# Rewriting the work order of a latent-attention and retention stage, and moving its rotations from VectorE to GpSimd

## The chip, the cores and the metric

The kernel runs on one core of a Trainium2 chip. The metric is the time of one execution in microseconds (us); the median of three executions of the kernel before is 1068.57 us (1067.65 to 1068.61). In the rows PE is TensorE, PEld its weight loads, DVE VectorE, ACT ScalarE, POOL GpSimd and SP the engine that issues most DMAs.

## The reference

The reference runs one sequence of 256 rows by 1024 features through seven pieces: a convolution mixer, a feed-forward, a sliding-window attention, two feed-forwards, a mixed stage, and a last feed-forward with a final norm. The change lies in the mixed stage:

```python
n = rms_norm(h, mix_norm[l])
proj = n @ w_in[l]
c_q, c_kv, k_pe, r_q, r_k, r_v, r_g = jnp.split(proj, SPLIT_POINTS, axis=-1)
a = mla_group(c_q, c_kv, k_pe, ...)     # 8 heads, softmax over 256 keys
r = retention_group(r_q, r_k, r_v, r_g, ...)  # 8 heads, decay in place of softmax
h = h + jnp.concatenate([a, r], axis=-1) @ w_o[l]
```

`mla_group` projects a latent of 256 + 128 features to queries, keys and values, rotates a part of them, and does softmax attention. `retention_group` rotates its queries and keys (the first half of every head times cosine and sine, minus and plus the second), multiplies scores by a decay, normalises each head over its features and gates the result.

## The kernel before

**Products.** The 256 rows are two tiles t = 0, 1 of 128. All weights come as one stream of chunks of 128 x 1024 floats (512 KB). Every product is exact to f32 by three passes: a chunk is split into a high part (ACT, `split_high`, L1044) and a low part (DVE, `split_low`, L1326), and so is the activation. Tile 0 multiplies a chunk first and waits for its split; tile 1 multiplies it last and frees its slot.

**Ring and raw buffers.** Split chunks live in a ring of 12 slots (`RING`), unsplit ones in 4 raw buffers (`RAW`). Once the chunk of a slot is freed, a step `R` splits the chunk that comes 12 later into it. SP loads a raw buffer again as soon as DVE has split what was in it, so at most four chunks are loaded ahead of the splits.

**Order.** Nothing is scheduled at run time. `walk` names the steps in one order, each engine walks through it and takes the steps that it has a part in, and works them off strictly in that order; semaphores join the engines. Where a step stands in `walk_latent` so decides what it stands behind on each of its engines. `freed` is the list of freed chunks, `refill(step, freed, n)` puts n steps `R` there.

**The head loop** (before: 797.5 to 831.3 us of the span). The MLA heads go in 8 pairs v:

- MS(v): PE multiplies the scores into bank pG[v % 2] (L1914); DVE takes the row maximum `mx` from there (L1576) and scales it to `negm` (L1579).
- ME(v): ACT takes the exponent into `mp` (L1249), two instructions with a sum each.
- MN(v): DVE takes the reciprocal of the sums (L1584) and multiplies `mp` by it (L1586).
- MPT(v): PE turns `mp` into bank pT (L1661), ACT copies it to `mpT` (L1256).
- MPV(v): PE multiplies it with the values (L1933).

Beside them run projections X(i, t, c), six matmuls of 128x512 each (L1656 to L1658): i = 3 are the retention's values, i = 4 its gate. VC takes the mean of the values (reduction on DVE, subtraction on POOL, L1000), `decay` makes the decay tables (ACT, POOL L1005), MAT splits the attention's output, RT turns the rotated queries and keys.

**The rest of the stage.** RS, RM and RPV are the retention's scores, their product with the decay (DVE, L1612) and the product with the values; SQ, VAR, GNvar, GNout the norm; GT turns the gate; RY multiplies it in (DVE `yo`, L1632; ACT splits off the high part), RL gives the low part (DVE, L1642). O(t, kt) are the output products, eight for each tile; O(t, 4..7) need RL(t). RROPE(t, part) is one rotation of 128 x 512 (part 0 queries, 1 keys): on DVE four multiplications into `ttmp` and two additions back into `rqk` (L1544 to L1550).

**The last feed-forward** takes blocks b: G(t, b) is the gate and up product over four chunks, T(t, b) turns the activated tile, D(t, b) is the down product over two. After T(0, 0) stands a refill of everything still in `freed`.

Of the kernel before, what the change touches and what calls it, by code (L numbers as in the profile page):

```python
# [31 lines left out]
ALU = mybir.AluOpType  # L32
# [3 lines left out]
P = 128  # L36
# [113 lines left out]
def refill(step, freed, n=None):  # L150

    for _ in range(len(freed) if n is None else min(n, len(freed))):
        step("R", freed.pop(0), 1, 0)
# [255 lines left out]
def walk_latent(step, freed, open_end):  # L409


    def project(i, t, c):
        step("X", i, t, c)
        if t == 1:
            freed.append(C_X[i] + c)

    def projects(i, t, cs=range(4)):
        for c in cs:
            project(i, t, c)
            if t == 1 and len(freed) > 1:  # L420
                refill(step, freed, 1)
# [30 lines left out]
    projects(3, 0)  # L452
    step("MT", 1)
    step("VC", 0)
# [3 lines left out]
    beside = [(3, 1, c) for c in range(1, 4)] + [(4, 0, c) for c in range(4)] + [(4, 1, 0)]  # L458
    project(*beside.pop(0))
    step("ME", 0)  # L460
    for v in range(1, 9):
        step("MN", v - 1)
        if v < 8:
            step("MS", v)
        refill(step, freed, v % 2)
        if v < 8:
            step("MPT", v - 1)
            project(*beside.pop(0))
            step("ME", v)
        else:  # L470
            step("RT", 0)
            step("MPT", v - 1)
            project(4, 1, 1)
        if v == 4:
            step("VC", 1)
        if v % 2 == 0:
            step("decay", v // 2 - 1)
        step("MPV", v - 1)
        if v == 7:
            step("MAT", 0)  # L480
    step("gate", 0)
    step("RT", 1)
    step("decay", 4)
    project(4, 1, 2)
    refill(step, freed, 1)
# [3 lines left out]
    project(4, 1, 3)  # L489
    refill(step, freed, 1)  # L490
# [5 lines left out]
    output(0, 0)  # L496
    refill(step, freed, 1)
# [5 lines left out]
    output(0, 1)  # L503
    step("MAT", 1)
    refill(step, freed, 1)
# [4 lines left out]
    output(0, 2)  # L510
    refill(step, freed, 1)
# [3 lines left out]
    step("SQ", 1)  # L515
    refill(step, freed, 1)
    output(0, 3)
    step("VAR", 1)
    step("GNvar", 1)
    step("GNout", 0)  # L520
    output(1, 0)
    refill(step, freed, 1)
    step("GNout", 1)
    output(1, 1)
    step("GT", 0)
    step("RY", 0)
    output(1, 2)
    step("RL", 0)
    step("GT", 1)
    step("RY", 1)  # L530
    output(1, 3)
    step("RL", 1)
    refill(step, freed, 4)
# [60 lines left out]
def build(nc, x_in, stream, consts_in, table_in, pos_in, posts_in, out):  # L594
    with ExitStack() as ctx:
# [172 lines left out]
        dm_exp, dm_ready = sem("dm_exp"), sem("dm_ready")  # L768
# [105 lines left out]
        def _(pool):  # L874
# [126 lines left out]

            def decay(hd, ph):

                pool.wait_ge(dm_exp, 3 * (hd + 1))
                pool.tensor_tensor(dm[hd][:, P:2 * P], dm[hd][:, P:2 * P], dtmp[hd % 2][:], ALU.mult).then_inc(dm_ready, 1)  # L1005
# [15 lines left out]
            steps = {f.__name__: f for f in (start, parts, finish, tail, rope, S, LAT, VC, decay, GNvar)}  # L1021
# [289 lines left out]
        def _(ve):  # L1311
# [218 lines left out]
            def RROPE(t, part, ph):  # L1530

                if t == 0 and part == 0:
                    ve.wait_ge(sincos_ready, 2)
                ve.wait_ge(x_out[t], 2 + part)
                z = rqk[t][:, 512 * part:512 * part + 512].rearrange("p (a f) -> p a f", f=HD)
                co, si = (x[:, t, :].unsqueeze(1).broadcast_to([P, 8, RHALF]) for x in (cos2, sin2))
                x1, x2 = z[:, :, 0:RHALF], z[:, :, RHALF:HD]
                if t or part:
                    ve.wait_ge(rrope_done[t if part else 0], 1 if part else 2)
                rotate(x1, x2, co, si, [x[:] for x in ttmp]).then_inc(rrope_done[t], 1)  # L1540

# [98 lines left out]
            def RL(t, ph):  # L1640
# [5 lines left out]
                         rope=rope, QKT=QKT, S=S, N=N, AT=AT, LAT=LAT, U=U, RROPE=RROPE, MT=MT, MS=MS, MN=MN, VC=VC, RT=RT, RM=RM, GNvar=GNvar, GNout=GNout,  # L1646
# [483 lines left out]
```

## Time and profile before

| what | value |
|---|---|
| median of three executions | 1068.57 us |
| the profiled execution's own time | 1068.61 us |
| its span, first to last instruction | 1066.8 us |
| PE busy / PE weight loads busy | 99% / 81% of the span |
| DVE / ACT / POOL busy | 62% / 53% / 8% |
| mean granted TensorE clock | 0.997 of full speed |
| HBM read | 186 MB, 175 GB/s over the span |

A busy share of PE is the time in which any matmul is in flight; matmuls overlap, so a wait shows only where PE has run dry. In a timeline a group xN is N instructions of one form, its duration from the first start to the last end. A bracket such as [1.39 <-DVE mp L1586] says that the engine sat idle 1.39 us and that this instruction released it.

### The profile page before, as it was taken

Reading aid. Unit: us, or ns where it says so; the run is one execution under the profiler, and the core shown is the slowest. Engines: PE = TensorE matmul, PEld = TensorE weight load, DVE = VectorE, ACT = ScalarE, POOL = GpSimd, SP = SyncE. Lnnn points to the kernel's source line nnn. Section 1 sums busy time; section 2 is a strip of 40 time slices with the busy share of each in tenths; the row PEclk is TensorE's granted clock in tenths of the full one; section 3 lists DMA queues with packets and bytes.
Section 4 is the critical chain, followed back from the end, with each engine's and each line's share of the span. In section 5 each row is a group of like instructions: output and inputs, shape, how many; then the busy total and the mean of one; then the engine's idle time right before and its main releaser. Section 6 shows DMA issues by size and latency. Waiting matters only on the chain.

```text
span 1066.8 us, 14789 instructions
## 1 busy us (share of the span) xinstructions
PE 1050.9 (99%) x5023; PEld 862.2 (81%) x5023; DVE 658.3 (62%) x956; ACT 566.7 (53%) x917; POOL 83.4 (8%) x170
## 2 busy tenths in 40 slices
PE   9999999999999999999999999999999999999997
PEld 6998888888877788888888888888886688888886
DVE  5867754645787765454576545466696664655544
ACT  5755644544677754454465445445567744444542
POOL 0034000000022040000000000000011110000001
PEclk9999999999999999999999999999999999999999
DMA  8573655546562364654656455565542353646541
GB/s 339 190 240 120 222 172 198 191 163 218 176 212 85 119 203 165 204 186 168 215 180 202 160 210 180 174 211 183 178 158 80 119 168 109 209 164 217 169 147 40
DMA packets 51883, 187.80 MB, mean 176 GB/s; under 512 B 5808, under 2 KB 5952, under 8 KB 51840
## 3 DMA queue, kind: packets, MB, share of 16 engines
q1 hardware_dynamic: 50688, 183.79, 51.0%
q0 software_dynamic: 864, 3.07, 1.0%
q8 instruction: 27, 0.44, 0.2%
q10 hardware_dynamic: 288, 0.37, 0.1%
q14 instruction: 16, 0.13, 0.0%
HBM read 186.15 MB, written 1.05 MB: 175 GB/s over the span
## 4 chain that ended last, share of the span: by engine, by line
PE 90%; DVE 6%; ACT 2%; issue 1%; POOL 0%; POOLq 0%; DVEq 0%; ACTq 0%
PE pG L1656 17%; PE pG L1658 17%; PE pG L1657 17%; PE pD L1656 11%; PE pD L1658 11%; PE pD L1657 11%; PE pT L1661 3%; DVE w_low L1326 2%; PE pG L1678 1%; PE pG L1661 1%; PE pT L1799 1%; PE pG L1914 0%; PE pD L1661 0%; ACT w_high L1044 0%; PE pD L1667 0%
## 5 line engine op out<-in xcount | busy, mean ns | idle before, releaser
L1326 DVE TENSOR_TENSOR w_low<-raw,w_high 128x1024 fp32r<-128x1024 f32 x340 | 410.8, 1225 | 121.6 <-ACT w_high L1044 108.1
L1044 ACT ACTIVATE w_high<-raw 128x1024 fp32r<-128x1024 f32 x340 | 352.8, 1055 | 76.7 <-PE pG L1658 66.2
L1656 PE MATMUL pG<-w_high,xTh 128*128 128x512 f32 (+1 forms) x816 | 319.9, 392 | 0.1
L1658 PE MATMUL pG<-w_high,xTl 128*128 128x512 f32 (+1 forms) x816 | 312.5, 383 | 0.0
L1657 PE MATMUL pG<-w_low,xTh 128*128 128x512 f32 (+1 forms) x816 | 312.1, 382 | 0.0
L1658 PEld LDWEIGHTS pG<-w_high,xTl 128*128 128x128 f32 x816 | 153.1, 188 | 28.0
L1657 PEld LDWEIGHTS pG<-w_low,xTh 128*128 128x128 f32 x816 | 153.6, 188 | 25.6
L1656 PEld LDWEIGHTS pG<-w_high,xTh 128*128 128x128 f32 x816 | 153.2, 188 | 25.6 <-DVE xTl L1359 0.3
L1656 PE MATMUL pD<-w_high,aTh 128*128 128x512 f32 x384 | 150.8, 393 | 0.0
L1658 PE MATMUL pD<-w_high,aTl 128*128 128x512 f32 x384 | 149.9, 390 | 0.0
L1657 PE MATMUL pD<-w_low,aTh 128*128 128x512 f32 x384 | 149.4, 389 | 0.0
L1129 ACT ACTIVATE gate<-pG,stat 128x256 f32<-128x256 f32 x104 | 49.3, 475 | 166.1 <-PE pG L1658 165.4
L1149 ACT ACTIVATE aTh<-pT 128x256 fp32r<-128x256 f32 x88 | 33.7, 383 | 150.7 <-PE pT L1661 150.7
L1465 DVE TENSOR_TENSOR aTl<-pT,aTh 128x256 fp32r<-128x256 f32 x88 | 37.4, 425 | 119.0 <-ACT aTh L1149 119.0
L1446 DVE SCALAR_TENSOR_TENSOR act<-pG,stat,gate 128x256 f32<-128x256 f32 x88 | 42.4, 481 | 94.8 <-ACT gate L1129 94.6
L1658 PEld LDWEIGHTS pD<-w_high,aTl 128*128 128x128 f32 x384 | 72.1, 188 | 15.1
L1657 PEld LDWEIGHTS pD<-w_low,aTh 128*128 128x128 f32 x384 | 72.2, 188 | 14.1
L1656 PEld LDWEIGHTS pD<-w_high,aTh 128*128 128x128 f32 x384 | 72.1, 188 | 14.1
L1656 PE MATMUL pD<-w_high,xTh 128*128 128x512 f32 (+1 forms) x160 | 65.5, 409 | 1.1 <-issue 1.1
L1658 PE MATMUL pD<-w_high,xTl 128*128 128x512 f32 (+1 forms) x160 | 62.6, 391 | 0.0
L1657 PE MATMUL pD<-w_low,xTh 128*128 128x512 f32 (+1 forms) x160 | 62.3, 390 | 0.0
L1656 PEld LDWEIGHTS pD<-w_high,xTh 128*128 128x128 f32 x160 | 30.2, 189 | 10.0 <-issue 4.9
(266 smaller groups left out, 811.5 us busy)
## 6 DMA issues: line engine op xcount, KB each, us to landing
raw<-in_stream SPq DMA_DIRECT2D x340, 512.0 KB, 4.4
post<-in_posts POOLq DMA_DIRECT2D x5, 512.0 KB, 4.8
early<-in_stream SPq DMA_DIRECT2D x4, 512.0 KB, 12.4
first_w<-in_stream SPq DMA_DIRECT2D x3, 512.0 KB, 5.9
h<-in_x SPq DMA_DIRECT2D x2, 512.0 KB, 5.5
out<-hg SPq DMA_DIRECT2D x3, 256.0 KB, 2.3
consts<-in_consts POOLq DMA_DIRECT2D x1, 417.0 KB, 4.5
out<-hg ACTq DMA_DIRECT2D x1, 256.0 KB, 2.7
```

What stands on the lines that cost most here:

```text
L1044: sc.activation(w_high[:, slot(static):slot(static) + CHUNK], raw_of(static), ACT.Copy).then_inc(w_high_done, 1)
L1129: sc.activation(gate[t][:], pG[t][:, 0:256], ACT.Copy if ph.mixer else ACT.Silu, scale=rr[t]).then_inc(gate_ready[t], 1)
L1149: sc.activation(aTh[t][:].rearrange("p k r -> p (k r)"), pT[t][:, 0:256], ACT.Copy).then_inc(ah_ready[t], 1)
L1326: ve.tensor_tensor(w_low[:, slot(static):slot(static) + CHUNK], raw_of(static), w_high[:, slot(static):slot(static) + CHUNK].bitcast(F32), ...
L1446: ve.scalar_tensor_tensor(act[t][:], pG[t][:, 256:512], rr[t], gate[t][:], ALU.mult, ALU.mult).then_inc(act_ready[t], 1)
L1465: ve.tensor_tensor(aTl[t][:].rearrange("p k r -> p (k r)"), pT[t][:, 0:256], aTh[t][:].rearrange("p k r -> p (k r)").bitcast(F32), ALU.sub ...
L1656: pe.matmul(dst, ah, hi, start=start, stop=False)
L1657: pe.matmul(dst, ah, lo, start=False, stop=False)
L1658: return pe.matmul(dst, al, hi, start=False, stop=stop)
L1661: return pe.transpose(dst, src, ident)
L1678: mm = pe.matmul(pG[t][:, 0:MIX.cols], hg[t][:, kt * P:(kt + 1) * P], first_w[:, kt * MIX.cols:(kt + 1) * MIX.cols], start=kt == 0, stop=k ...
L1799: mm = pe.matmul(pT[p][:, P * keys * x:P * keys * (x + 1)], qT[t][part, 4 * a + first + x, :], kT[part, a, 0:P * keys], start=True, stop=True)
```

## The change

The change has five parts.

1. RROPE moves from DVE to POOL, 24 instructions with the same operands. The wait for the sine and cosine tables on DVE goes with it.
2. In the head loop MS runs two pairs ahead of MN and MPT, where it ran one ahead. PE's round was MS(v), MPT(v-1), X, MPV(v-1); it is MPT(v), X, MS(v+2), MPV(v-1). A second refill stands ahead of the loop, before MN(0), and the first VC before the second MT. X(4, 1, 0) and X(4, 1, 1) leave the loop.
3. The retention part is ordered anew: three projections beside RT, RS and RPV, RL(0) after both RY, VAR(1) followed by O(0, 3).
4. There the refills are fewer: two single ones and one of two, where there were seven single ones and one of four (three were left to do). What is left over moves behind T(0, 0) of the last feed-forward.
5. A semaphore `rot_part` counts POOL's four multiplications.

```diff
--- before.py
+++ after.py
@@ -450,87 +450,85 @@
     step("exp_table",)
     freed += [C_U, C_U + 1, C_U + 2]
     projects(3, 0)
+    step("VC", 0)
     step("MT", 1)
-    step("VC", 0)
     project(3, 1, 0)
     refill(step, freed, 1)
     step("MS", 0)
-    beside = [(3, 1, c) for c in range(1, 4)] + [(4, 0, c) for c in range(4)] + [(4, 1, 0)]
+    step("ME", 0)
+    step("MS", 1)
+    beside = [(3, 1, c) for c in range(1, 4)] + [(4, 0, c) for c in range(4)]
     project(*beside.pop(0))
-    step("ME", 0)
-    for v in range(1, 9):
-        step("MN", v - 1)
-        if v < 8:
-            step("MS", v)
+    refill(step, freed, 1)
+    for v in range(8):
+        if v < 7:
+            step("ME", v + 1)
+        step("MN", v)
+        step("MPT", v)
+        for _ in range(min(1, len(beside))):
+            project(*beside.pop(0))
+        if v < 6:
+            step("MS", v + 2)
+        if v >= 1:
+            step("MPV", v - 1)
+        if v == 3:
+            step("VC", 1)
+        if 2 <= v < 6:
+            step("decay", v - 2)
+        if v == 6:
+            step("MAT", 0)
         refill(step, freed, v % 2)
-        if v < 8:
-            step("MPT", v - 1)
-            project(*beside.pop(0))
-            step("ME", v)
-        else:
-            step("RT", 0)
-            step("MPT", v - 1)
-            project(4, 1, 1)
-        if v == 4:
-            step("VC", 1)
-        if v % 2 == 0:
-            step("decay", v // 2 - 1)
-        step("MPV", v - 1)
-        if v == 7:
-            step("MAT", 0)
+    step("RT", 0)
     step("gate", 0)
+    step("MPV", 7)
+    project(4, 1, 0)
     step("RT", 1)
+    project(4, 1, 1)
     step("decay", 4)
-    project(4, 1, 2)
-    refill(step, freed, 1)
     step("decay", 5)
     step("RS", 0)
     step("RM", 0)
-    project(4, 1, 3)
-    refill(step, freed, 1)
+    project(4, 1, 2)
     step("decay", 6)
     step("RPV", 0)
     step("RS", 1)
     step("RM", 1)
     step("decay", 7)
-    output(0, 0)
-    refill(step, freed, 1)
+    project(4, 1, 3)
     step("RPV", 1)
     step("RS", 2)
     step("gate", 1)
     step("SQ", 0)
     step("RM", 2)
-    output(0, 1)
     step("MAT", 1)
-    refill(step, freed, 1)
+    output(0, 0)
     step("RPV", 2)
     step("RS", 3)
     step("RM", 3)
     step("silu",)
-    output(0, 2)
-    refill(step, freed, 1)
+    output(0, 1)
     step("VAR", 0)
     step("GNvar", 0)
     step("RPV", 3)
     step("SQ", 1)
+    step("GNout", 0)
     refill(step, freed, 1)
-    output(0, 3)
+    output(0, 2)
     step("VAR", 1)
     step("GNvar", 1)
-    step("GNout", 0)
-    output(1, 0)
+    output(0, 3)
+    step("GNout", 1)
     refill(step, freed, 1)
-    step("GNout", 1)
-    output(1, 1)
+    for kt in range(3):
+        output(1, kt)
     step("GT", 0)
     step("RY", 0)
-    output(1, 2)
-    step("RL", 0)
+    output(1, 3)
     step("GT", 1)
     step("RY", 1)
-    output(1, 3)
+    step("RL", 0)
     step("RL", 1)
-    refill(step, freed, 4)
+    refill(step, freed, 2)
     for kt in range(4, 8):
         output(0, kt)
     step("tail", 0, C_INDEX)
@@ -765,7 +763,7 @@
...
@@ -999,6 +997,22 @@
                 z = rv[t][:].rearrange("p (a f) -> p a f", f=HD)
                 pool.tensor_tensor(z, z, gn[t][:, 0, :].unsqueeze(2).broadcast_to([P, RET_HEADS, HD]), ALU.subtract).then_inc(vc_ready, 1)
 
+            def RROPE(t, part, ph):
+
+                pool.wait_ge(x_out[t], 2 + part)
+                z = rqk[t][:, 512 * part:512 * part + 512].rearrange("p (a f) -> p a f", f=HD)
+                co, si = (x[:, t, :].unsqueeze(1).broadcast_to([P, 8, RHALF]) for x in (cos2, sin2))
+                x1, x2 = z[:, :, 0:RHALF], z[:, :, RHALF:HD]
+                if t or part:
+                    pool.wait_ge(rrope_done[t if part else 0], 1 if part else 2)
+                pool.tensor_tensor(ttmp[0][:], x1, co, ALU.mult).then_inc(rot_part, 1)
+                pool.tensor_tensor(ttmp[1][:], x2, si, ALU.mult).then_inc(rot_part, 1)
+                pool.tensor_tensor(ttmp[2][:], x1, si, ALU.mult).then_inc(rot_part, 1)
+                pool.tensor_tensor(ttmp[3][:], x2, co, ALU.mult).then_inc(rot_part, 1)
+                pool.wait_ge(rot_part, 4 * (2 * t + part + 1))
+                pool.tensor_tensor(x1, ttmp[0][:], ttmp[1][:], ALU.subtract)
+                pool.tensor_tensor(x2, ttmp[2][:], ttmp[3][:], ALU.add).then_inc(rrope_done[t], 1)
+
             def decay(hd, ph):
 
                 pool.wait_ge(dm_exp, 3 * (hd + 1))
@@ -1018,7 +1032,7 @@
                 pool.wait_ge(end_m, 2)
                 pool.tensor_tensor(rr[1], ms[1], half_neg[:, 0:1], ALU.pow).then_inc(end_r, 1)
 
...
 
             def step(name, *args, ph=None):
@@ -1527,18 +1541,6 @@
                 ve.wait_ge(lath_ready, t + 1)
                 ve.tensor_tensor(latTl[:], latf[:], latTh[:].bitcast(F32), ALU.subtract).then_inc(latT_ready, 1)
 
-            def RROPE(t, part, ph):
-
-                if t == 0 and part == 0:
-                    ve.wait_ge(sincos_ready, 2)
-                ve.wait_ge(x_out[t], 2 + part)
-                z = rqk[t][:, 512 * part:512 * part + 512].rearrange("p (a f) -> p a f", f=HD)
-                co, si = (x[:, t, :].unsqueeze(1).broadcast_to([P, 8, RHALF]) for x in (cos2, sin2))
-                x1, x2 = z[:, :, 0:RHALF], z[:, :, RHALF:HD]
-                if t or part:
-                    ve.wait_ge(rrope_done[t if part else 0], 1 if part else 2)
-                rotate(x1, x2, co, si, [x[:] for x in ttmp]).then_inc(rrope_done[t], 1)
-
             def rotate(x1, x2, co, si, tmp):
 
                 chain(ve.tensor_tensor(tmp[0], x1, co, ALU.mult))
@@ -1643,7 +1645,7 @@
                                  xTh[t][:, 4:8, :].rearrange("p k r -> p (k r)").bitcast(F32), ALU.subtract).then_inc(catT_ready[t], 1)
 
...
 
```

What this does to the instructions is shown at three places. Names carry the buffer's digit (pG0, mp1) and a running number.

DVE at the start of the head loop, before: the maximum of pair 0 (from pG0), MN(0), the maximum of pair 1, and the chunk split after it.

```order
L1576 TENSOR_REDUCE mx0_67<-pG0 128x2 [waits ms_psum]
L1579 TENSOR_SCALAR negm0_69<-mx0_67 128x2 [waits ve_chain]
L1584 RECIPROCAL lrec0_73<-lsum0_71 128x2 [waits mp_ready]
L1586 TENSOR_TENSOR mp0_133<-mp0_133,lrec0_73 128x512 [waits ve_chain]
L1576 TENSOR_REDUCE mx0_67<-pG1 128x2 [waits ms_psum]
L1579 TENSOR_SCALAR negm0_69<-mx0_67 128x2 [waits ve_chain]
L1326 TENSOR_TENSOR w_low_51<-raw_49,w_high_50 128x1024 [waits w_high_done]
L1584 RECIPROCAL lrec0_73<-lsum0_71 128x2 [waits mp_ready]
```

DVE at the same place, now:

```order
L1578 TENSOR_REDUCE mx0_67<-pG0 128x2 [waits ms_psum]
L1581 TENSOR_SCALAR negm0_69<-mx0_67 128x2 [waits ve_chain]
L1578 TENSOR_REDUCE mx0_67<-pG1 128x2 [waits ms_psum]
L1581 TENSOR_SCALAR negm0_69<-mx0_67 128x2 [waits ve_chain]
L1340 TENSOR_TENSOR w_low_51<-raw_49,w_high_50 128x1024 [waits w_high_done]
L1586 RECIPROCAL lrec0_73<-lsum0_71 128x2 [waits mp_ready]
L1588 TENSOR_TENSOR mp0_133<-mp0_133,lrec0_73 128x512 [waits ve_chain]
L1578 TENSOR_REDUCE mx0_67<-pG0 128x2 [waits ms_psum]
L1581 TENSOR_SCALAR negm0_69<-mx0_67 128x2 [waits ve_chain]
```

MN(0), which is RECIPROCAL and mp0, stood behind one maximum; now it stands behind two and behind a chunk split, and MN(1) will stand behind the maximum of pair 2.

PE around MPT(2) (pT0 from mp0), before: MPV(1), MS(3), MPT(2).

```order
L1933 MATMUL pD0<-mpT1_137,mv0_125 64x128 [waits mpT_ready]
L1933 MATMUL pD0<-mpT1_137,mv0_125 64x128
L1933 MATMUL pD0<-mpT1_137,mv1_126 64x128 x2
L1914 MATMUL pG1<-mkT_120,mqT_117 128x256 [waits mp_ready]
L1914 MATMUL pG1<-mkT_120,mqT_117 128x256
L1661 MATMUL pT0<-consts_61,mp0_133 128x128 [waits mpT_ready,mn_ready]
L1661 MATMUL pT0<-consts_61,mp0_133 128x128 x3
```

PE at the same place, now: MS(3), MPV(0), MPT(2).

```order
L1916 MATMUL pG1<-mkT_120,mqT_117 128x256 [waits mp_ready]
L1916 MATMUL pG1<-mkT_120,mqT_117 128x256
L1935 MATMUL pD0<-mpT0_136,mv0_125 64x128 [waits mpT_ready]
L1935 MATMUL pD0<-mpT0_136,mv0_125 64x128
L1935 MATMUL pD0<-mpT0_136,mv1_126 64x128 x2
L1663 MATMUL pT0<-consts_61,mp0_133 128x128 [waits mpT_ready,mn_ready]
L1663 MATMUL pT0<-consts_61,mp0_133 128x128 x3
```

MS(3) and MPT(2) are as close as before. What the rows alone don't say is that on DVE MN(2) stood before the maximum of pair 3 and now stands behind it.

DVE at the start of the last feed-forward, before: the preparation of tile 1, T(0, 0), one chunk split, and the activation of G(0, 1).

```order
L1359 TENSOR_TENSOR xTl1_55<-hg1_85,xTh1_53 128x512 [waits xh_ready1] x2
L1465 TENSOR_TENSOR aTl0_80<-pT0,aTh0_78 128x256 [waits ah_ready0]
L1326 TENSOR_TENSOR w_low_51<-raw_49,w_high_50 128x1024 [waits w_high_done]
L1446 SCALAR_TENSOR_TENSOR act0_88<-pG0,stat_63,gate0_86 128x256 [waits gate_ready0]
L1465 TENSOR_TENSOR aTl0_80<-pT0,aTh0_78 128x256 [waits ah_ready0]
```

DVE at the same place, now:

```order
L1373 TENSOR_TENSOR xTl1_55<-hg1_85,xTh1_53 128x512 [waits xh_ready1] x2
L1479 TENSOR_TENSOR aTl0_80<-pT0,aTh0_78 128x256 [waits ah_ready0]
L1340 TENSOR_TENSOR w_low_51<-raw_49,w_high_50 128x1024 [waits w_high_done] x7
L1460 SCALAR_TENSOR_TENSOR act0_88<-pG0,stat_63,gate0_86 128x256 [waits gate_ready0]
L1479 TENSOR_TENSOR aTl0_80<-pT0,aTh0_78 128x256 [waits ah_ready0]
```

Seven chunk splits stand between T(0, 0) and the activation of G(0, 1), where one stood.

## Rows read from the trace of the kernel before

**Rows 1.** The page, part 1: busy us, share of the span and instructions of each engine.

```profile
PE 1050.9 (99%) x5023; PEld 862.2 (81%) x5023; DVE 658.3 (62%) x956; ACT 566.7 (53%) x917; POOL 83.4 (8%) x170
```

**Rows 2.** The waits of PE, 740 to 900 us: us in total, times, longest.

```profile
PE pT L1661 <- DVE mp L1586: 3.0, 3, 1.4
PE pD L1656 <- issue: 1.1, 1, 1.1
PE pT L1973 <- DVE sd L1612: 0.7, 1, 0.7
PE pG L1656 <- DVE mkT L1570: 0.6, 1, 0.6
```

**Rows 3.** Stretches: length; busy us by engine; granted clock, DMA share, GB/s.

```profile
797.50:831.30 33.80, 30.84 (x190) 22.63 (x190) 22.39 (x43) 21.84 (x60) 4.79 (x6) 1.00 0.24 79
```

**Rows 4.** Timeline of PE, head loop: start, us, work, idle before.

```profile
802.24 0.66 PE L1661 MATMUL pT<-consts,mp 128*128 128x128 f32 x4 [1.39 <-DVE mp L1586]
...
804.21 0.66 PE L1933 MATMUL pD<-mpT,mv 128*64 128x128 f32 x8
804.80 1.13 PE L1914 MATMUL pG<-mkT,mqT 96*128 96x256 f32 x4
...
807.70 0.66 PE L1933 MATMUL pD<-mpT,mv 128*64 128x128 f32 x8
```

**Rows 5.** Timeline of DVE over the same rounds.

```profile
801.29 0.17 DVE L1584 RECIPROCAL lrec<-lsum 128x2 f32<-128x2 f32 x1 [1.09 <-ACT mp L1249]
801.49 0.69 DVE L1586 TENSOR_TENSOR mp<-mp,lrec 128x512 f32<-128x512 f32 x1
802.10 0.68 DVE L1576 TENSOR_REDUCE mx<-pG 128x2 f32<-128x512 f32 x1
802.82 0.17 DVE L1579 TENSOR_SCALAR negm<-mx 128x2 f32<-128x2 f32 x1
802.90 1.22 DVE L1326 TENSOR_TENSOR w_low<-raw,w_high 128x1024 fp32r<-128x1024 f32 x1
...
805.97 0.69 DVE L1576 TENSOR_REDUCE mx<-pG 128x2 f32<-128x512 f32 x1 [0.60 <-PE pG L1914]
```

**Rows 6.** Timeline of ACT over the same rounds.

```profile
800.24 0.47 ACT L1249 ACTIVATE mp<-pG,negm 128x256 f32<-128x256 f32 x1 [3.02 <-DVE negm L1579]
...
801.15 1.05 ACT L1044 ACTIVATE w_high<-raw 128x1024 fp32r<-128x1024 f32 x1
802.93 0.60 ACT L1256 ACTIVATE mpT<-pT 128x512 f32<-128x512 f32 x1 [0.73 <-PE pT L1661]
```

**Rows 7.** Timeline of POOL, 797 to 818 us.

```profile
798.23 1.95 POOL L1000 TENSOR_TENSOR rv<-rv,gn 128x512 f32<-128x512 f32 x1 [15.54 <-DVE gn L1594]
...
815.88 1.04 POOL L1000 TENSOR_TENSOR rv<-rv,gn 128x512 f32<-128x512 f32 x1 [4.96 <-DVE gn L1594]
```

**Rows 8.** Timeline of DVE beside the second of these.

```profile
816.29 1.17 DVE L1586 TENSOR_TENSOR mp<-mp,lrec 128x512 f32<-128x512 f32 x1
```

**Rows 9.** Tile ttmp, one of six lines of a rotation: ns min/median/max.

```profile
L1544 DVE TENSOR_TENSOR ttmp<-rqk,trig x4: 413/418/419, 760.0 to 793.8; 128x256 f32<-128x256 f32 x4
```

**Rows 10.** Timeline of DVE before the last product of the stage.

```profile
860.00 0.69 DVE L1642 TENSOR_TENSOR xTl<-yo,xTh 128x512 fp32r<-128x512 f32 x1 [0.70 <-ACT xTh L1303]
860.61 0.68 DVE L1632 TENSOR_TENSOR yo<-roS,pG 128x512 f32<-128x512 f32 x1
```

**Rows 11.** Timeline of PE, 856 to 858 us.

```profile
856.77 0.63 PE L1657 MATMUL pD<-w_low,xTh 128*128 128x512 f32 x1
857.20 0.63 PE L1658 MATMUL pD<-w_high,xTl 128*128 128x512 f32 x1
```

**Rows 12.** Timeline of PE at the start of the last feed-forward.

```profile
880.15 0.44 PE L1661 MATMUL pT<-consts,act 128*128 128x128 f32 x2 [0.21 <-DVE act L1446]
```

**Rows 13.** Timeline of DVE at the same place.

```profile
883.82 1.23 DVE L1326 TENSOR_TENSOR w_low<-raw,w_high 128x1024 fp32r<-128x1024 f32 x1 [0.52 <-ACT w_high L1044]
```

**Rows 14.** Tile raw, 775 to 790 us: from a load's issue to its landing.

```profile
DMA to landing us min/median/max: 3.3/4.4/5.2
```

More of the change, by code:

```diff
@@ L767, in build @@
         rT_psum, rqT_ready, rkT_ready = sem("rT_psum"), sem("rqT_ready"), sem("rkT_ready")
-        dm_exp, dm_ready = sem("dm_exp"), sem("dm_ready")
+        dm_exp, dm_ready, rot_part = sem("dm_exp"), sem("dm_ready"), sem("rot_part")
         rs_psum, sd_ready, rpv_done = sem("rs_psum"), sem("sd_ready"), sem("rpv_done")
@@ L1019, in finish @@
                 pool.tensor_tensor(rr[1], ms[1], half_neg[:, 0:1], ALU.pow).then_inc(end_r, 1)
-            steps = {f.__name__: f for f in (start, parts, finish, tail, rope, S, LAT, VC, decay, GNvar)}
+            steps = {f.__name__: f for f in (start, parts, finish, tail, rope, S, LAT, VC, RROPE, decay, GNvar)}
             in_loop = ("G", "D", "T", "Y", "R")
@@ L1645, in _ @@
             steps = dict(start=start, fill=fill, R=refill, turn=turn, parts=parts, second=second, finish=finish, tail=tail, join=join, G=G, T=T, Y=Y,
-                         rope=rope, QKT=QKT, S=S, N=N, AT=AT, LAT=LAT, U=U, RROPE=RROPE, MT=MT, MS=MS, MN=MN, VC=VC, RT=RT, RM=RM, GNvar=GNvar, GNout=GNout,
+                         rope=rope, QKT=QKT, S=S, N=N, AT=AT, LAT=LAT, U=U, MT=MT, MS=MS, MN=MN, VC=VC, RT=RT, RM=RM, GNvar=GNvar, GNout=GNout,
                          MAT=MAT, RY=RY, RL=RL)
```

## The prediction

> **What bounds the kernel now.** I read the page's busy shares first: PE is in flight for 99% of the span, everything else for at most 81% [rows 1]. A change that leaves PE's matmuls as they are, as this one does, can only take away or add waits of PE, so I read next who PE waited for around the stage. From 740 to 900 us that is 5.4 us in all: 3.0 for the normalised probabilities of MN in the head loop, 1.1 put down to issue (the wait of O(1, 0) for the first value of the norm, a DVE result that VAR(1) had just asked for), 0.7 for RM, 0.6 for `mkT` [rows 2]. That is all that the new order can win. Then I read the timelines of PE, DVE and ACT over two rounds of the head loop, to see how much room stands between a result and its use.
>
> The round takes 3.49 us (804.21 to 807.70) [rows 4]. After MS(v) the chain is: maximum, exponent, MN, MPT. The maximum starts 1.17 us after MS does (804.80, 805.97) [rows 4, 5]; DVE's next instruction starts 0.80 us after it (802.10 to 802.90) [rows 5]; the exponents start at 800.24 and leave ACT free 0.91 us later; MN's reciprocal starts at 801.29, 1.05 us after the exponents, and MPT 0.95 us after it [rows 4 to 6]. The old order hides this chain nearly whole because DVE does MN(v-1) before it must wait for MS(v).
>
> **The head loop.** The new PE round is MPT(v), X, MS(v+2), MPV(v-1), MPT(v+1). On ACT the distance of two pairs does what it seems to do, the exponents are early. But DVE works in program order, and there MN(v+1) stands behind the maximum of pair v+2, which waits for MS(v+2) of the same PE round. So a round is:
>
> - MPT and X, 1.97 us (802.24 to 804.21) [rows 4]
> - MS(v+2) to its maximum, 1.1 us (an estimate: the 1.17 of above, less what PE loses in changing over from an MPV, which MS no longer follows)
> - the maximum to the next DVE instruction, 0.80; reciprocal to MPT(v+1), 0.95 [rows 4, 5]
>
> That is 4.83 us, with 0.6 of it covered by MPV(v-1) on PE. When a refill stands between the two (v = 1, 3, 5), add the step of a chunk split, 1.22 less the 0.08 by which DVE's instructions overlap: 5.97 us. The high part on ACT is ready for it, but for v = 1, where ACT copies the values first (0.15). For v = 3 VC adds 0.79, and its subtraction on POOL another 0.6 (below).
>
> Ahead of the loop: MS(0) at 0, maximum at 1.1 to 1.17, exponents from 2.1, ACT free at 3.0, the high part of the extra refill until 4.1, its low part on DVE until 5.25, MPT(0) at 6.2. Rounds v = 0, 2, 4: 3 x 4.83 = 14.5. Rounds 1, 3, 5: 3 x 5.97 + 0.15 + 0.79 + 0.6 = 19.45. From MPT(6) to MPT(7) nothing is left to multiply, and MAT stands before MN(7) on DVE: copy visible after 0.69 (802.24, 802.93) [rows 4, 6], two ACT copies 1.1, DVE 0.61, MN 0.95, together 3.35. MPT(7) is so at 43.5. MPT, MPV(6), RT and MPV(7) add 2.5, and two X that the old loop held, 3.1: 49.1 against 33.8 of the old stretch with the same work [rows 3]. **Term A: +15.3 us.** It hangs on no duration that the trace lacks, only on the order. Its ends: without the lock and with chunk splits that DVE finds time for, 11; with splits that come late from ACT, 18.
>
> **The retention part.** Gone are the issue wait (VAR(1) is followed by O(0, 3), 1.5 us of work), RM's wait (no split stands before RM(0)), and the low-clock stretch that followed VAR: there matmuls start every 0.43 us (856.77, 857.20) [rows 11] where 0.23 is usual, so that X takes 2.6 and not 1.4 to 1.6; eight matmuls and the turn beside them cost 1.4. New is a wait before O(0, 4): its low part RL(0) now stands behind RY(1), which waits for GT(1). From GT(1): 0.69 to `yo`, 0.61 to the next instruction, 0.69 for RL [rows 10], 2.0 in all, with 0.4 of GT on PE: 1.6. **Term B:** -1.1 - 0.7 - 1.4 + 1.6 = **-1.6 us** (-3.2 if the low part is early, 0 if the clock falls here again).
>
> **The rotations.** DVE is rid of 24 instructions of 0.42 us [rows 9], 10 us. That frees the one place where they bind: U(1) waits 0.6 for `mkT`, whose copies stood behind a rotation and four splits. POOL's cost for 128x256 isn't in the trace. The nearest row is 1.04 us for 128x512 with two inputs [rows 7]; half of that, 0.52, and the whole are the ends, and I take 0.7. A rotation is then 4.2 us (3.1 to 6.2). The last starts when `rqk` of tile 1 is out, near 787, and is over by 795; its first readers are ME(1), after 800, and RT. So it is covered. The cost is elsewhere. POOL's subtraction took 1.95 us beside DVE and 1.04 alone, and the DVE product beside the second took 1.17 where 0.69 is usual [rows 5, 7, 8]: the two wait for each other. The last rotation so meets DVE's U(1), on which MT(1) waits; at most two of its six instructions should fall on it. **Term C:** -0.6 (-1 to +3.6).
>
> The Trainium skill has a rule that speaks against this part: in SBUF — State Buffer, "SBUF: two separate sides", the port pair of VectorE and GpSimd is an exclusive lock, held for a whole instruction, that a VectorE instruction with two SBUF inputs needs. The trace agrees (1.17 against 0.69). By it alone, what moved to POOL gives DVE nothing back wherever DVE is busy.
>
> **The last feed-forward.** G(0, 1) starts after the turn at 880.15, at about 880.35 [rows 12]. It needs chunks 4 to 7 of the phase, a chunk each 1.4 us (six matmuls). Now only chunk 4 is split by then; 5 to 11 come behind T(0, 0). The first split there starts at 883.82 [rows 13] and is done at 885.05, where PE wants it at 881.75: 3.3 us. The next come each 1.14 and keep up. But only four loads run ahead: the load of chunk 9 waits for the split of 5, lands 3.3 to 4.4 later [rows 14], and with two split steps of 1.05 and 1.22 is ready at 891 to 892, wanted at 890.6. And the activation of G(0, 1) stands behind all seven on both engines: the last is split near 893.5, T(0, 1) could start at 892.3 to 893. That gives 0.4 to 1.4 and 1.4 more. **Term D: +5.5 us** (5 to 6.2; 2 if loads land sooner). Behind it the ring is as full as it was.
>
> **The clock.** The granted clock fell once in this stage, to 1.2 of 2.4 GHz, after VAR's small matmuls and the wait of 1.1 us, and an X in it cost 1.2 more [rows 2, 11]. The waits of 1.4 in the loop did not make it fall. The new waits are longer and closer: 2.9, 2.1, 2.8, 1.5, 4.0, 1.5, 2.7 and 2.4 in the loop, 3.3 at the end. I take it that the longest four or five each cost such a stretch, and that in each about 0.9 falls on the path. **Term E: +4 us** (0 to +10).
>
> **Sum.** 15.3 - 1.6 - 0.6 + 5.5 + 4 = 22.6 on the profiled execution's 1068.6 (span 1066.8 and 1.8 around it, the median of the runs is the same to 0.1): 1091.2, said as 1091.
>
> **The rivals.**
>
> - *Scores two ahead hide the softmax after all.* For it speaks that MS and its MPT lie two rounds apart. The 3.0 go, with B and C that is -5.2, and D gives 5.5 back: 1068.9; with D at nothing, 1063. It needs that MN(v+1) doesn't wait for MS(v+2), so it decides at one point: whether DVE starts a reciprocal before the maximum that stands ahead of it. In the trace no DVE instruction does so. The Trainium skill says the same of VectorE (TensorE: Matmul & The Clock Gate, "Architectural detail: the array is 16× 32×32, not 1× 128×128": its queue is strictly first in, first out). Chance 0.05.
> - *The rotations on POOL bind.* If each of the six instructions of the last rotation holds DVE's U(1) up, MT(1) is 4.2 late and C is +3.6, and those beside the splits delay a chunk: 1096 to 1097. Chance 0.12.
> - *The clock stays low.* If every wait brings a low stretch, nine of them at 1.2, E is 10 to 11: 1098. Chance 0.12.
> - *The splits find room.* If ACT's high parts come while DVE waits for MS, the odd rounds cost 4.83: A falls by 3.4, and with E near 1 it is 1085. But a split behind the maximum can't start before it. Chance 0.04.
>
> **How the numbers follow.** The forecast's own case has 0.67, around 1091. With A at 11 and E at 0 it is 1083, and a little less with D at 5: 1082 is the low end. 1099 takes in the second and third rival. What a measurement here can tell from no change is about 0.2%, 2 us. Faster needs the first rival without D: 0.03; within 0.2%, the same with D: 0.02; slower 0.95.
>
> **What would show it.** MPT of the head loop should wait for DVE `mp` eight times, 18 to 20 us in total, rounds alternating near 4.8 and 6.0; the loop up to RT(0) should take about 44.5 us at full clock. A wait of 1.6 before O(0, 4) for `xTl` L1644. At the last feed-forward, PE waits for `w_low` about 3.3 us, then for `act` 1.4. The granted clock below 0.95 in the loop. POOL's rotation instructions 0.5 to 1.9 us, no wait of PE for `rqk`. I am wrong if the loop's waits are near 3 us in all, or if PE waits for `w_low` nowhere.

## The result and the profile after

The changed kernel takes 1096.84 us (median of four runs, 1096.28 to 1097.33) against 1068.59 (1067.65 to 1069.51): a ratio of 1.0264, 95% interval 1.0247 to 1.0282, so 28 us slower. The forecast was 1091 with a range of 1082 to 1099. The direction and the mechanism of the head loop held, and the sum was 5.6 us short. The experiments below are mostly about these 5.6.

First the page of the changed kernel: its span, part 1, and the granted clock in 40 slices.

```profile
span 1095.3 us, 14788 instructions
PE 1059.1 (97%) x5023; PEld 867.6 (79%) x5023; DVE 658.3 (60%) x932; ACT 567.8 (52%) x917; POOL 105.1 (10%) x194
PEclk9999999999999999999999999999988999999999
```

The work is that of before [rows 1], but for 24 instructions that went from DVE to POOL. DVE's busy time didn't fall with them. The waits of PE from 740 to 930 us, which answer to [rows 2]:

```profile
PE pT L1663 <- DVE mp L1588: 17.5, 8, 3.8
PE pG L1658 <- DVE w_low L1340: 3.1, 1, 3.1
PE pT L1663 <- DVE act L1460: 2.3, 2, 2.1
PE pG L1663 <- DVE mq L1552: 1.7, 1, 1.7
PE pD L1658 <- DVE xTl L1644: 1.4, 1, 1.4
```

These are 26.0 us where before there were 5.6 (the 5.4 of [rows 2] and 0.2 ahead of T(0, 0)). From kernel to kernel MT(0) starts up to 1.5 us earlier or later, behind work that the edits don't touch, so I compare distances between landmarks and not positions. In the timeline of PE, these rows are the landmarks:

```profile
777.90 0.60 PE L1663 MATMUL pG<-consts,mq 128*96 128x128 f32 x4
...
799.36 1.96 PE L1916 MATMUL pG<-mkT,mqT 96*128 96x256 f32 x8
...
851.67 0.60 PE L1658 MATMUL pD<-w_high,xTh 128*128 128x512 f32 x1
...
882.81 0.50 PE L1658 MATMUL pD<-w_high,xTh 128*128 128x512 f32 x1 [1.38 <-DVE xTl L1644]
...
901.41 0.44 PE L1663 MATMUL pT<-consts,act 128*128 128x128 f32 x2 [0.21 <-DVE act L1460]
...
906.35 0.67 PE L1658 MATMUL pG<-w_high,xTh 128*128 128x512 f32 x1 [3.11 <-DVE w_low L1340]
...
917.13 0.44 PE L1663 MATMUL pT<-consts,act 128*128 128x128 f32 x2 [2.08 <-DVE act L1460]
```

They are MT(0), MS(0), the first X after MPV(7), O(0, 4), T(0, 0), G(0, 1) and T(0, 1). The same landmarks in the other kernels:

| stretch, us | before | after | clock kept up and late splits gone (`e8`) | new order (`e7`) |
|---|---|---|---|---|
| MT(0) to MS(0) | 20.4 | 21.5 | 21.4 | 20.4 |
| MS(0) to the end of the head loop, equal work | 33.8 | 55.4 | 48.6 | 31.3 |
| from there to T(0, 0) | 48.8 | 46.6 | 47.5 | 45.2 |
| T(0, 0) to T(0, 1) | 8.5 | 15.7 | 8.5 | 8.5 |

(To make the work of the loop equal, 1.55 us are added to it and taken from the next stretch for each X that a kernel does behind it: two after and in `e8`, one in `e7`. Where RT(1) or an X follows MPV(7), its start and the end of MPV(7) differ by up to 0.1 us.) The column after, less the column before, is 1.1 + 21.6 - 2.2 + 7.2 = 27.7; the other 0.8 of the difference of the spans lies ahead of MT(0). Behind T(0, 1) both take 178.2.

The lock that was forecast can be read off DVE's timeline, here where the clock is full:

```profile
808.45 0.69 DVE L1578 TENSOR_REDUCE mx<-pG 128x2 f32<-128x512 f32 x1 [3.00 <-PE pG L1916]
809.17 0.17 DVE L1581 TENSOR_SCALAR negm<-mx 128x2 f32<-128x2 f32 x1
809.25 0.16 DVE L1586 RECIPROCAL lrec<-lsum 128x2 f32<-128x2 f32 x1
809.44 0.69 DVE L1588 TENSOR_TENSOR mp<-mp,lrec 128x512 f32<-128x512 f32 x1
```

The exponents for this reciprocal were done at 804.3, but DVE stood idle for 3.00 us in front of the maximum of pair 2, behind which the reciprocal of pair 1 stands. And at half clock, on PE:

```profile
818.86 0.63 PE L1659 MATMUL pD<-w_low,xTh 128*128 128x512 f32 x1
819.28 0.63 PE L1660 MATMUL pD<-w_high,xTl 128*128 128x512 f32 x1
```

A matmul starts every 0.43 us, as in [rows 11]. The stretch from MS(0) to the end of MPV(7), in a view of stretches (length; busy us by engine; granted clock, DMA share, GB/s):

```profile
799.36:851.67 52.31, 34.81 (x179) 25.95 (x179) 22.55 (x42) 23.92 (x61) 4.18 (x5) 0.84 0.15 51
```

The mean of 0.84 says that the clock was at its half level for about a third of the loop; finer stretches show four pieces.

### The profile page after: what moved, and what is told of

Same layout as the page of the kernel before. It is cut to its first block, busy times and chain, and to the rows that moved or that the text cites. A ratio compares the mean times of both kernels' runs of the same rounds, so it can differ in the third digit from the quotient of the medians.

```text
span 1095.3 us, 14788 instructions
## 1 busy us (share of the span) xinstructions
PE 1059.1 (97%) x5023; PEld 867.6 (79%) x5023; DVE 658.3 (60%) x932; ACT 567.8 (52%) x917; POOL 105.1 (10%) x194
## 3 DMA queue, kind: packets, MB, share of 16 engines
q1 hardware_dynamic: 50688, 183.79, 49.4%
## 4 chain that ended last, share of the span: by engine, by line
PE 89%; DVE 7%; ACT 2%; issue 1%; DMA 1%; POOL 0%; POOLq 0%; ACTq 0%; DVEq 0%; SPq 0%
PE pG L1658 16%; PE pG L1660 16%; PE pG L1659 16%; PE pD L1658 11%; PE pD L1660 10%; PE pD L1659 10%; DVE w_low L1340 3%; PE pT L1663 3%; PE pG L1680 1%; PE pG L1663 1%; ACT w_high L1058 1%; PE pG L1916 1%; PE pT L1801 1%; DVE mp L1588 1%; DMA raw<-in_stream 1%
## 5 line engine op out<-in xcount | busy, mean ns | idle before, releaser
L1663 PE MATMUL pT<-consts,act 128*128 128x128 f32 x192 | 37.9, 271 | 2.3 <-DVE act L1460 2.3
## 6 DMA issues: line engine op xcount, KB each, us to landing
early<-in_stream SPq DMA_DIRECT2D x4, 512.0 KB, 12.6
```

The source lines that it names most:

```text
L1663: return pe.transpose(dst, src, ident)
```

## The experiments

Ratios are against the kernel before, with a 95% interval. Line numbers shift by a few between the kernels.

### One part undone, or done alone

**The rotations on DVE again (`e1`)**, all else as changed: `RROPE` moved back from POOL's steps to DVE's, word for word as the diff has it.

> The changed kernel with one part undone: the rotations of the retention's queries and keys (RROPE) are on DVE again. My theory, from the trace of the changed kernel: beside these rotations POOL stretched four low parts of DVE from 1.2 to 1.7 us and two products of U(1) from 0.3 to 0.8, and MT(1) came 1.7 us late; in the kernel before it waited 0.6 for another thing. So 1.9 us are given back: 1096.8 becomes 1095 (1094 to 1096), the 1.7 us wait for mq is gone and the wait of 0.6 for mkT is back. Rival, the term C of my prediction (the part wins 0.6): the time rises to 1097.4. A second rival: the late start is the order of VC(0) and MT(1), not POOL; then nothing changes and the wait for mq stays.

Measured: 1097.06 us (1095.05 to 1099.57), ratio 1.0264 (1.0247 to 1.0281). The times can't tell it from the changed kernel, since they scatter by 4.5 us here (below). Its trace can. First DVE in the changed kernel, then in this one:

```profile
783.77 6.78 DVE L1340 TENSOR_TENSOR w_low<-raw,w_high 128x1024 fp32r<-128x1024 f32 x4 [0.16 <-ACT w_high L1058]
...
793.59 0.82 DVE L1547 TENSOR_TENSOR mpT<-mq,trig 128x128 f32<-128x128 f32 x1
794.34 0.81 DVE L1548 TENSOR_TENSOR mpT<-mq,trig 128x128 f32<-128x128 f32 x1
```

```profile
787.47 4.62 DVE L1324 TENSOR_TENSOR w_low<-raw,w_high 128x1024 fp32r<-128x1024 f32 x4
...
793.17 0.29 DVE L1543 TENSOR_TENSOR mpT<-mq,trig 128x128 f32<-128x128 f32 x1
793.37 0.29 DVE L1544 TENSOR_TENSOR mpT<-mq,trig 128x128 f32<-128x128 f32 x1
```

So the stretching is as I had said: 2.2 us on four splits, 0.5 on each product that meets POOL. But MT(0) to MS(0) goes from 21.5 to 21.1 only, not to 19.6. PE waits for `mkT` twice now, 0.6 and 0.8 us; the second wait is new, since the change also put VC(0) ahead of MT(1), and without POOL's delay that order costs something itself (`e7`, with the rotations on DVE and MT(1) first, has one wait of 0.6 and 20.4 us). My expectation of 1.9 was wrong.

**The rotations on POOL in the kernel before (`e2`).** The same function, moved the other way.

> The kernel before with one part of the change alone: RROPE on POOL. By the same theory PE waits about 1.7 us for mq before MT(1) and no longer 0.6 for mkT, and 1068.6 becomes 1070 (1069.5 to 1071). The rival of term C (it wins 0.6 and costs nothing): 1068.0. If what moved to POOL gave DVE real time back in the head loop too, it would be under 1067.

Measured: 1069.70 us (1068.58 to 1071.48, twelve runs), ratio 1.0010 (1.0001 to 1.0019): +1.1 us. MT(0) to MS(0) is 21.4 against 20.4, with the wait of 1.7 for `mq` in place of 0.6 for `mkT`. This part of the change costs 1 us; the rival that it wins 0.6 falls.

**The old head loop in the changed kernel (`e3`):** the lines of before from MS(0) to MPV(7) in place of the new ones, with X(4, 1, 0) and X(4, 1, 1) in them as before.

> The changed kernel with the head loop of before (up to RT(0)) put back, the rest as changed. My theory: the loop holds 14.9 us of waits at full clock and 6.8 us lost to four stretches at half clock that those waits bring with them; both go, and 5.2 us at the last feed-forward stay, perhaps 1 more since one refill fewer stands in the loop: 1076 (1074 to 1078), with PE waits of 3 us in the loop and the granted clock at 1.00 there. Rival: the retention part and the rotations are what brings the low clock, and the loop only costs its waits: then four us or more of half clock stay and it is 1081 or above.

Measured: 1076.35 us (1076.12 to 1076.98), ratio 1.0069 (1.0054 to 1.0084), as expected. The loop is back to 33.2 us, with 2.3 us of waits for `mp`. Its stretch:

```profile
798.76:831.96 33.20, 30.91 (x191) 22.72 (x192) 21.60 (x41) 21.91 (x60) 2.92 (x5) 1.00 0.24 80
```

The clock stays at 1.00 there and in the retention part, so the rival falls. Two waits of PE at the last feed-forward:

```profile
PE pG L1654 <- DVE w_low L1336: 4.5, 1, 4.5
PE pT L1659 <- DVE act L1456: 1.2, 2, 1.0
```

The old loop does one split fewer, so eight and not seven stand behind T(0, 0); the first wait is 4.5 us and not 3.1, and the clock falls in it and stays low for a while behind it.

### The lock

**MN(v+1) ahead of MS(v+2) (`e4`)**, the only edit:

```diff
     for v in range(8):
         if v < 7:
             step("ME", v + 1)
-        step("MN", v)
+        if v == 0:
+            step("MN", 0)
         step("MPT", v)
         for _ in range(min(1, len(beside))):
             project(*beside.pop(0))
+        if v < 7:
+            step("MN", v + 1)
         if v < 6:
             step("MS", v + 2)
```

> The changed kernel with one line moved: MN(v+1) is asked for ahead of MS(v+2), so that on DVE the normalisation stands in front of the maximum that waits for the next scores; scores still run two pairs ahead. My theory (it is the order on DVE alone that locks the loop): the eight waits for mp, 17.5 us, fall under 3 us, PE's clock stays at 1.00 in the loop, and the loop takes no more than the old one: 1073 to 1077. Rival (the exponents and copies on ACT, or the chunk splits, are what comes late, whatever the order on DVE): waits of 10 us or more stay, and the time is 1085 or above.

Measured: 1078.40 us (1077.66 to 1082.18), ratio 1.0085 (1.0070 to 1.0100). This one edit gives 18.4 us back. The trace is that of the slowest of its four executions (1082.18 us; the others took 1077.66 to 1078.92). PE in its steady rounds, MPT to MPT in 3.42 us, and then DVE in the same rounds:

```profile
815.13 0.66 PE L1666 MATMUL pT<-consts,mp 128*128 128x128 f32 x4
817.00 1.03 PE L1919 MATMUL pG<-mkT,mqT 96*128 96x256 f32 x4
817.96 0.66 PE L1938 MATMUL pD<-mpT,mv 128*64 128x128 f32 x8
818.55 0.65 PE L1666 MATMUL pT<-consts,mp 128*128 128x128 f32 x4
```

```profile
816.75 0.16 DVE L1589 RECIPROCAL lrec<-lsum 128x2 f32<-128x2 f32 x1
816.95 0.69 DVE L1591 TENSOR_TENSOR mp<-mp,lrec 128x512 f32<-128x512 f32 x1
818.07 0.69 DVE L1581 TENSOR_REDUCE mx<-pG 128x2 f32<-128x512 f32 x1 [0.43 <-PE pG L1919]
```

`mp` is ready 0.9 us before its MPT. It missed my range by 1.4 us all the same. Waits of 4.8 are left and not under 3; the largest, 2.81, is that of MPT(0), since ahead of the loop there is still one product too few and a split in front of MN(0), and the clock still fell twice. With that, the loop takes 39.5 us for equal work in this execution, and not the 33.8 of before, as I had expected. The rival (ACT or the splits are what is late, whatever the order) would have kept 10 us of waits, and falls. The edit does more than its name says, though: MN(v+1) now also goes ahead of what stood between it and the maximum, a split in rounds 1, 3 and 5, VC in round 3, MAT in round 6. What each of these cost is read from `e8` below.

### The last feed-forward

**The splits in the retention part again (`e5`)**, where the change left four: five times `+    refill(step, freed, 1)` behind its products, and the last `refill(step, freed, 2)` back to 4. The edit asks for eleven, as the expectation says, but one step finds no freed slot, and the trace shows ten (six, and four in a row). The kernel before does eleven, four of them in its last refill and not three.

> The changed kernel with the refills of the retention part put back (eleven chunk splits there instead of four), its head loop and all else as changed. My theory: at the last feed-forward PE waits 3.1 us for a low part, 2.1 for the activation behind seven splits, and loses 2 us to a stretch at half clock that follows; all of it goes, and RM or another short wait may come back with up to 0.7: 1096.8 becomes 1090 (1089 to 1091.5), with no wait of PE for a low part of a chunk. Rival: the late chunks only hide a loss that stands there anyway, since the loads share the ring; then it is 1094 or above and a wait of over 2 us for a low part is left, now earlier.

Measured: 1091.09 us (1090.02 to 1094.49), ratio 1.0205 (1.0189 to 1.0220), within the range. T(0, 0) to T(0, 1) is 8.5 us, and no wait for a split is left. An issue wait of 0.8 comes instead. The loop of this kernel is that of the changed one, and yet from MS(0) to RT(0) it took 52.8 us in the profiled execution, against 49.4 in the changed kernel; the clock was low for longer there. So the time that the low clock costs is not one number for one order: in its four runs the mean clock lay between 0.985 and 0.992, and the slowest had the lowest.

### The clock

**Work added in the waits (`e6`).** Ahead of its wait, each MPT does matmuls of no use:

```diff
             def MPT(v, ph):
+                for _ in range((14, 8, 15, 4, 20, 4, 11, 10)[v]):
+                    pe.matmul(pD[1][:, 896:1024], ident, ident, start=True, stop=True)
                 pe.wait_ge(mn_ready, v + 1)
```

> The changed kernel with work added and nothing removed: ahead of its wait for mn_ready every MPT(v) on PE does 14, 8, 15, 4, 20, 4, 11 or 10 small matmuls (128 by 128 of the identity into columns of PSUM that the last MPV overwrites), which fill the waits but for about half a microsecond each. No data and no order changes. My theory, that 6.8 us of the loop's loss are the low clock and that PE's standing still is what brings it: the clock stays at 1.00 in the loop and the time falls by about 6.8 although PE has more to do: 1090 (1089 to 1092). Rival 1 (the low clock hangs on something else than PE's waits, or the filler isn't seen as work): the clock falls as often as before, and it is 1096 to 1099. Rival 2 (the rounds are long by DVE's chain alone and the low clock beside them costs nothing): the clock stays up and the time stays at 1096 to 1097.

Measured: 1092.15 us (1091.07 to 1093.09), ratio 1.0215 (1.0199 to 1.0230). PE does 86 matmuls more and the kernel is 4.7 us faster, just beside my range. The stretch from MS(0) to the end of MPV(7):

```profile
798.76:846.09 47.33, 47.12 (x351) 40.62 (x351) 21.22 (x41) 23.26 (x61) 4.17 (x5) 1.00 0.17 57
```

The clock stays at 1.00. The filling was somewhat too long: `mp` was ready 1.1 us before MPT(2) came, 0.8 before MPT(4) and 0.2 before three others. With the shorter filling of `e8` 1.4 of the 2.1 us that were missing to 1090 are won. Both rivals fall: the clock stayed up with the filling, and the low clock had a price.

**Shorter filling and the splits of `e5` together (`e8`)**, with `(13, 8, 11, 4, 17, 4, 10, 9)[v]`.

> The changed kernel with two causes taken away at once: the eleven splits of the retention part are back, and the waits of MPT in the head loop are filled with 13, 8, 11, 4, 17, 4, 10 and 9 small matmuls (0.23 us each; where the first filling was too long by 1.1, 0.8 and three times 0.2 us it is shorter). What is left of the change then is the locked loop at full clock, the rotations on POOL and the retention part. My theory, that the terms add: 1096.8 less 7.2 at the last feed-forward, less 5.1 that the first filling won, less 2 that it was too long by: 1082.5 (1081 to 1084), with the loop from MS(0) to RT(0) in 43.5 to 44.5 us. Rival: the shorter filling leaves gaps in which the clock falls again, or the splits bring new waits; then it is 1085 or above.

Measured: 1083.53 us (1083.32 to 1083.75), ratio 1.0137 (1.0121 to 1.0152). That is 1.0 above the 1082.5 to which the terms added and within the range, and the runs now lie within 0.5 us of each other. The same stretch:

```profile
799.01:844.48 45.47, 45.26 (x331) 38.48 (x331) 21.25 (x41) 23.26 (x61) 4.17 (x5) 1.00 0.18 59
```

45.5 us against 52.3 with the low clock. This is the locked loop at full clock, and in it the rounds stand as they were forecast:

| MPT(v) to MPT(v+1), v = | 0 | 1 | 2 | 3 | 4 | 5 | 6 |
|---|---|---|---|---|---|---|---|
| forecast | 4.83 | 6.12 | 4.83 | 7.36 | 4.83 | 5.97 | 3.35 |
| `e8`, full clock | 4.69 | 5.98 | 4.64 | 7.33 | 4.63 | 5.83 | 3.36 |
| after | 4.69 | 7.43 | 6.28 | 7.26 | 6.27 | 5.83 | 3.36 |

In rounds 0, 2 and 4 of `e8` nothing stands between the maximum and MN, and they take 1.2 us more than the 3.42 of `e4`. By that, an estimate, the maximum alone accounts for about 7.4 of the 12.6 us by which rounds 0 to 5 are longer than six of 3.42. The other 5.2 are the splits and VC, which ran hidden in `e4` and stand in the chain here.

### A version that follows

**The new order (`e7`)**: the changed loop with the order of `e4`, and besides: two products between MS(1) and MPT(0) and no split there, the other five after MPT(v) for v = 0, 1, 2, 4, 6, RT(0) ahead of MPT(7), the rotations on DVE, MT(1) ahead of VC(0), VAR(1) followed by O(0, 3), RL(0) ahead of GT(1), X(4, 1, 0) behind MPT(7), one split in each of rounds 0, 1, 2, 4 and 6, and ten splits in the retention part. An excerpt, against the changed kernel:

```diff
+    project(*beside.pop(0))
     project(*beside.pop(0))
-    refill(step, freed, 1)
     for v in range(8):
...
+        if v == 7:
+            step("RT", 0)
         step("MPT", v)
-        for _ in range(min(1, len(beside))):
+        if v in (0, 1, 2, 4, 6):
             project(*beside.pop(0))
...
```

> A version that follows from the runs so far: scores two pairs ahead, MN(v+1) ahead of MS(v+2), two products between MS(1) and MPT(0) and no split there, the other five spread over the rounds, RT(0) ahead of MPT(7), the rotations on DVE, VAR(1) followed by O(0, 3), RL(0) ahead of GT(1), and eleven splits in the retention part. My theory: the waits of the old loop (3.0 us) go down to about 1, the issue wait of 1.1 and the stretch at half clock of 1.2 behind it go, and nothing comes at the last feed-forward: 1064.5 (1063 to 1067) against 1068.6 before. Rival: rounds without a product are shorter than the chain from a score to its MPT, so the waits only move, 3 us or more stay in the loop, and the clock may fall there: 1068 to 1072.

Measured: 1063.52 us (1063.33 to 1063.88), ratio 0.9950 (0.9937 to 0.9964): 5.1 us faster than the kernel before, and 33 faster than the changed one. All its waits of PE from 740 to 900 us:

```profile
PE pT L1671 <- DVE mp L1596: 1.3, 2, 0.8
PE pG L1666 <- DVE mkT L1580: 0.6, 1, 0.6
PE pT L1671 <- DVE act L1456: 0.2, 1, 0.2
```

**The same with the rotations on POOL (`e9`).**

> The version of the run before that was faster than both (1063.5), with one thing changed: the rotations of the retention on POOL. My theory: as in the two runs on this part, POOL stretches DVE's splits and U(1), PE waits 1.7 us for mq instead of 0.6 for mkT, and it is 1064.5 (1064 to 1065.5). Rival: DVE is the engine with less room in this loop, and ten microseconds of work less on it win more than they cost: 1063 or under.

Measured: 1064.37 us (1063.99 to 1064.67), ratio 0.9957 (0.9944 to 0.9971). That is 0.85 more, and MT(0) to MS(0) is 21.4 against 20.4 again. Every kernel with the rotations on POOL has this 1 us, whatever the loop behind it looks like.

**Two splits moved (`e10`)**: `if v in (0, 1, 5, 6)` in place of `(0, 1, 2, 4, 6)` ahead of the loop's `refill`. The loop has one split fewer by it, which the retention part then does.

> The same version with two splits moved in the head loop: none after rounds 2 and 4, in which the split stood ahead of the MN that PE then waited for (0.54 and 0.79 us), one after round 5, where DVE waits 1.1 us for the exponents; one split fewer in the loop in all. My theory: both waits go and nothing else comes: 1062.3 (1062 to 1063). Rival: the one split fewer comes back as a wait for a chunk at the last feed-forward: 1063.5 or above.

Measured: 1063.06 us (1061.80 to 1063.78), ratio 0.9945 (0.9931 to 0.9958). The waits for `mp` went from 1.3 to 0.9 us, not to nothing, and from MS(0) to T(0, 1) it is 84.62 us against 84.95. The gain of 0.3 to 0.5 is less than the scatter; whether it is faster than `e7` stays open.

## Why the prediction was right, and where it was short

| term | forecast | measured | how |
|---|---|---|---|
| A, the lock at full clock | +15.3 | +14.8 | loop of `e8`, 48.6 against 33.8 |
| B, the retention part | -1.6 | -2.2 | landmarks before and after |
| C, rotations on POOL | -0.6 | +1.0 | landmarks; ratio of `e2`; `e9` against `e7` |
| D, last feed-forward | +5.5 | +7.2 | T(0, 0) to T(0, 1), 15.7 against 8.5 |
| E, the clock | +4 | +6.8 | loop, 55.4 against 48.6 of `e8` |

The measured terms sum to 27.6. Three of mine were too low: E by 2.8 us, D by 1.7, C by 1.6; the others are within 0.6. D lies outside its own range of 5 to 6.2.

- **A held**, in its sum and round by round. The step that carries it, that MN(v+1) waits behind the maximum of pair v+2, is shown by DVE's idle 3.00 us and by `e4`: one step moved, 18.4 us back. The waits were forecast as 18 to 20 us and were 17.5. The Trainium skill's rule that VectorE's queue is strictly first in, first out (TensorE: Matmul & The Clock Gate, "Architectural detail: the array is 16× 32×32, not 1× 128×128") is what this case shows, with DVE idle for 3.00 us in front of a maximum while its next input had long been ready.
- **B held.** The issue wait, RM's wait and the low clock there are gone, and 1.38 (forecast 1.6) before O(0, 4) are new. That wait was avoidable: `e7`, with RL(0) ahead of GT(1), doesn't have it.
- **C failed at the step "at most two of its six instructions should fall on it".** I looked at the last rotation and at DVE's wide products. In fact the rotation before it stretched four splits by 2.2 us, about as much as a rotation on DVE takes, and the last one met even DVE's instructions of 0.17 us, which then took 0.7. Counted from MT(0), DVE began its part of U(1) 1.9 us earlier than in `e1` and ended it 1.1 us later. The rule of the Trainium skill that I had set beside this term was nearer than my count: in SBUF — State Buffer, "SBUF: two separate sides", the shared port pair is held for a whole instruction. The trace agrees: 0.82 us for a product that takes 0.29 alone. (The 1.04 us of [rows 7] that I had called alone lay beside DVE's product of 1.17; the value held, it is also 1.04 after the change, with DVE idle beside it.) With it the rival "the rotations on POOL bind" was right in kind, and at 3.6 us too dear.
- **D held in its first wait** (3.1 us, forecast 3.3) **and was too small behind it.** The step that was mis-sized is the load, "lands 3.3 to 4.4 later". These are pieces of the chain that ends in T(0, 1), start and length in us:

```profile
905.07 3.50 DVE w_low L1340 x3
...
908.74 5.61 DMA raw<-in_stream
...
914.37 1.07 ACT w_high L1058
...
915.46 1.22 DVE w_low L1340
916.68 0.41 DVE act L1460
```

The last chunk's load took 5.61 us, with the DMA engines busy for 0.95 of the time from 910 to 917.1; ACT waits 1.8, 1.2 and 1.4 us for the last three loads. So the wait for `act` is 2.1 and not 1.4, and the one of 0.4 to 1.4 for chunk 9 doesn't come, since PE is late itself. PE's clock was low here too (0.53 from 906.4 to 910.0), but from 900.4 to 917.1 no work of PE stands in this chain: at full clock PE would have waited longer for `act` instead, so this stretch did not cost the 2 us that the expectation of `e5` gave it. `e6` and `e4` repeat it, with 15.7 and 15.6 us and waits of 2.0 and 2.1.

- **E was mis-sized, and is the largest part of the miss.** The step was "the longest four or five each cost such a stretch, and in each about 0.9 falls on the path". The number of pieces was about right: four in the loop, the last of them twice as long as the others, and one at the last feed-forward that cost nothing. The share on the path was wrong. No row stood behind the 0.9, and I had thought of a kernel in which PE's products hide other work. In a locked round they hide nothing: MPT, X and MS(v+2) stand in one chain with DVE, so every matmul that runs slower adds its whole delay. The table of rounds shows it: 1.5, 1.6 and 1.6 us in three rounds, and 2.2 from MPT(7) to MPV(7).

Of the rivals, "the clock stays low" gave 1098 by nine stretches at 1.2. Its result is nearer than mine, by luck: the trace has four stretches that count, each dearer, and the rest of the difference is C and D. Scores two ahead do hide the softmax, as the first rival had it, but only in the order of `e4`, not in that of the change.

Open: what decides in which rounds the clock falls. The same loop lost 6.8 us to it in one profiled execution and some 3 more in another, and no run here tells why. B was not undone by itself; it rests on the landmarks and on the waits that are gone.

## What to carry to other kernels

Issuing work earlier on one engine doesn't shorten a chain if its result is asked for, on the next engine, ahead of the older result: write out the row of steps of every engine that the chain passes, and put the instruction whose input is ready in front of the one that must wait. A wait of the bounding engine costs more than its length when the clock falls behind it, and most where that engine's work is itself a link of the chain; price a low stretch there by the full delay of the matmuls in it, and at nothing where another chain ends later anyway. An engine that is rid of work gains nothing if the work goes to one that holds it up while it runs, so count the busy neighbours of every moved instruction, not the moved ones.

## What the runs showed of the hardware

Adding matmuls made the kernel faster: 86 of them in PE's waits, 1096.8 to 1092.2 us, by keeping the granted clock at 1.00. Waits of 1.4 us had not made it fall in the loop before [rows 4]; with waits of 1.2 to 3.8 in every round it was at half speed for about a third of the time. It varied between executions of one kernel (1090.0 to 1094.5 us in `e5`), and with the loop's waits filled as well that scatter went down to 0.4 us (`e8`); in `e6`, filled but with the late splits, it was 2.0. Loads of 512 KB that landed within 3.3 to 5.2 us of their issue before [rows 14] took up to 5.7 where seven splits in a row asked for them. A POOL product of 128x256 with two inputs takes 0.75 us where it goes first, and 1.72 where a chunk split of DVE goes first (DVE's four start at 783.77, above, just behind the first of these rows):

```profile
783.67 0.75 POOL L1010 TENSOR_TENSOR ttmp<-rqk,trig 128x256 f32<-128x256 f32 x1
784.37 1.72 POOL L1011 TENSOR_TENSOR ttmp<-rqk,trig 128x256 f32<-128x256 f32 x1
```
